# Gathering two experts' rows at once, channel-major, in a fused transformer step

## What is computed

```
def moe_ffn(h, w_rg, b_rg, w_re, b_re, w_gate, w_up, w_down):
    ...
    grp = jnp.argmax(logit_g, axis=-1)
    ...
    top_val, top_idx = lax.top_k(logit_e, TOP_K)
    weight = p_grp * jax.nn.softmax(top_val, axis=-1)
    ...
    def expert_block(args):
        tok, e, w = args
        xb = h_pad[tok]
        y = (jax.nn.silu(xb @ w_gate[e]) * (xb @ w_up[e])) @ w_down[e]
        return y * w[:, None]
```

## Time and profile before

| what | us |
|---|---|
| device time, median of 3 runs | 1075.61 |
| lowest and highest of the 3 | 1073.88, 1075.84 |
| span of the profiled execution, first to last instruction | 1073.9 |
| of it busy: TensorE matmuls | 1045.2 (97%) |
| VectorE, ScalarE, GpSimd | 285.9, 239.0, 91.3 |

### The profile page before, as it was taken

How to read it: one execution, slowest core, us unless ns; L and a number is a source line. 1 busy time by engine, 2 the same in 40 slices (tenths; PEclk the granted TensorE clock), 3 DMA queues, 4 the chain that set the end, 5 groups by cost and what they waited for, 6 DMA issues and landing times.

```text
span 1073.9 us, 14364 instructions
## 1 busy us (share of the span) xinstructions
PE 1045.2 (97%) x5798; PEld 537.2 (50%) x5798; DVE 285.9 (27%) x767; ACT 239.0 (22%) x492; POOL 91.3 (9%) x133
## 2 busy tenths in 40 slices
PE   8999999999999999999999999999999999999994
PEld 4478887555666667775543333333333333333342
DVE  1132011566333314111441111111111111122252
ACT  2011001266322243000131311111111111111153
POOL 0020040000222220000000000000000000000000
PEclk9999999999999999999999999999999999999997
DMA  9990248220545578654289999999999999999920
GB/s 330 259 300 6 79 99 177 79 80 1 168 146 160 186 272 193 248 192 161 78 329 392 379 425 426 426 428 428 427 428 427 427 428 428 426 427 424 371 73 31
DMA packets 58359, 288.93 MB, mean 269 GB/s; under 512 B 10211, under 2 KB 14540, under 8 KB 45566
## 3 DMA queue, kind: packets, MB, share of 16 engines
q1 hardware_dynamic: 48414, 259.61, 62.7%
q0 software_dynamic: 9648, 28.43, 9.1%
q10 hardware_dynamic: 240, 0.09, 0.0%
HBM read 277.87 MB, written 19.55 MB: 277 GB/s over the span
## 4 chain that ended last, share of the span: by engine, by line
PE 53%; DMA 8%; DVE 1%; issue 1%; ACT 0%; POOL 0%; SPq 0%; DVEq 0%; POOLq 0%
PE ps L1187 18%; PE ps L1215 9%; PE ps L601 9%; PE ps L1159 4%; DMA reg_o<-in_w_exp_down_dram 4%; DMA ring<-in_w_exp_up_dram 3%; PE ps L1084 3%; PE ps L672 2%; PE ps L1172 1%; PE ps L1163 1%; DMA late<-y_rows 1%; PE ps L1203 1%; PE ps L620 1%; PE ps L1055 1%; PE ps L679 1%
## 5 line engine op out<-in xcount | busy, mean ns | idle before, releaser
L1187 PE MATMUL ps<-ring,reg_xh 128*64 128x512 f32 x512 | 148.7, 595 | 2.5 <-DMA ring<-in_w_exp_up_dram 1.7
L1187 PE MATMUL ps<-late,reg_xh 128*64 128x512 f32 x336 | 148.6, 595 | 0.9 <-DMA reg_k<-in_w_exp_up_dram 0.9
L1187 PEld LDWEIGHTS ps<-ring,reg_xh 128*64 128x64 f32 x512 | 46.2, 137 | 86.9 <-issue 84.3
L2194 DVE TENSOR_TENSOR reg_xh<-reg_xh,ps 64x512 f32<-64x512 f32 x32 | 22.1, 691 | 230.4 <-ACT reg_xh L1592 230.4
L1592 ACT ACTIVATE reg_xh<-ps 64x512 f32<-64x512 f32 x32 | 34.0, 1064 | 215.0 <-PE ps L1187 215.0
L1187 PE MATMUL ps<-reg_k,reg_xh 128*64 128x512 f32 x176 | 77.8, 595 | 0.0
L2413 POOL DMA_INDIRECT y_rows<-reg_xh,slot_row x29 | 28.3, 976 | 544.4 <-ACT reg_xh L1603 503.2
L897 PE MATMUL ps<-reg_xh,ring 128*128 128x320 f32 x256 | 73.5, 436 | 0.0
L1187 PEld LDWEIGHTS ps<-late,reg_xh 128*64 128x64 f32 x336 | 44.4, 137 | 45.4 <-issue 44.9
L601 PE MATMUL ps<-reg_xh,ring 128*128 128x320 f32 x224 | 60.9, 433 | 0.0
L1159 PE MATMUL ps<-reg_xh 128*64 128x512 f32 x256 | 60.5, 592 | 0.0
(11 more groups left out here) (412 smaller groups left out, 1340.3 us busy)
## 6 DMA issues: line engine op xcount, KB each, us to landing
ring<-in_w_exp_gate_dram SPq DMA_DIRECT2D x21, 2048.0 KB, 19.4
ring<-in_w_in_dram SPq DMA_DIRECT2D x12, 2048.0 KB, 11.0
ring<-in_w_exp_down_dram SPq DMA_DIRECT2D x11, 2048.0 KB, 24.0
ring<-in_w_exp_up_dram SPq DMA_DIRECT2D x11, 2048.0 KB, 23.9
late<-in_w_exp_gate_dram SPq DMA_DIRECT2D x10, 2048.0 KB, 19.9
reg_k<-in_w_exp_up_dram SPq DMA_DIRECT2D x10, 2048.0 KB, 24.4
late<-in_w_exp_up_dram SPq DMA_DIRECT2D x10, 2048.0 KB, 23.4
reg_xh<-in_w_exp_down_dram SPq DMA_DIRECT2D x10, 2048.0 KB, 23.5
```

Source lines behind the costliest of these rows:

```text
L1187: last = pe.matmul(out[64 * part:64 * part + 64, :], xb[:, k, :], ws_[part][:, k, :], start=(k == 0), stop=(k == KT - 1))
L2194: dve.tensor_tensor(sg.rearrange("p (m q) -> p m q", m=4), sg.rearrange("p (m q) -> p m q", m=4), ps[64:128, 2 + par, :].rearrange("p (q m ...
```

## The change

The rows of two experts are gathered at once, and what was the stationary operand becomes the moving one: a block of 128 tokens x 128 channels of `xn2` is loaded, and the one-hot columns of two experts (2 x 64) stream through. The result is channel-major already, in PSUM banks 0 and 1 for both experts. `turn_rows`, the copy to `xg` and `add_rows` go. `pick` runs in every other step (par 0), before the whole of `down`, which is no longer split. VectorE builds the one-hot matrix of both experts in one instruction, into a single buffer. `times_gain` reads the two banks, one expert in each step. TensorE waits, ahead of `pick`, until both experts of the last pair have been taken out of the banks (`xe_ready`). The job `rank` moves to bank 7.

```
-    assign(proj, (1, 3, 4, 5, 2, 3))
+    assign(proj, (7, 3, 4, 5, 2, 3))
...
-            def gather(bufs, out, s_ready, count, s_done):
-
+            def pick(width, banks, s_ready, count, s_done):
 
                 pe.wait_ge(s_ready, count)
+
+                def chosen_rows(t, rows, c, m, **flags):
+
+                    c0, col = 512 * c + 128 * m, 256 * (m % 2) + 128 * c
+                    return pe.matmul(ps[:, banks[m // 2], col:col + width], xn2[rows, t, c0:c0 + 128],
+                                     sel[rows, t, :, :].rearrange("p q n -> p (q n)")[:, 0:width], **flags)
+
                 for t in range(2):
+                    for m in range(4):
+                        for c in range(2):
+                            chosen_rows(t, slice(0, 128), c, m, start=(t == 0 and m % 2 == 0 and c == 0), stop=False)
+                for m in range(2):
                     for c in range(2):
...
+                        chosen_rows(2, slice(0, 64), c, m, start=False, stop=(m == 1 and c == 1))
+                        last = chosen_rows(2, slice(64, 128), c, 2 + m, start=False, stop=(m == 1 and c == 1))
                 last.then_inc(s_done, 1)
...
-            gather(sel[0], ps[:, 0, :], sel_ready, 1, gathered)
+            pick(128, (0, 1), sel_ready, 1, picked)
             projected(1, 1)
-            pe.wait_ge(xg_added, 1)
-            turn_rows(xg_ready, 1, xg_turned)
             projected_sample()
...
-                if not last_one:
-                    gather(sel[1 - par], ps[:, 1 - par, :], sel_ready, e + 2, gathered)
+                if par == 0 and keep != 2:
+                    pe.wait_ge(xe_ready, e + 2)
+                    pick(128, (0, 1), sel_ready, i * 3 + p // 2 + 2, picked)
                 if first:
                     slot_table()
-                if not first:
-                    down(w_down, he[1 - par], ps[:, 5 - par, :], (0, 1))
-                if not last_one:
-                    pe.wait_ge(xg_added, e + 2)
-                    turn_rows(xg_ready, e + 2, xg_turned)
-                if first:
                     pe.wait_ge(sg_ready, 1)
                 else:
-                    down(w_down, he[1 - par], ps[:, 5 - par, :], (2, 3), e + 1).then_inc(down_done, 1)
+                    down(w_down, he[1 - par], ps[:, 5 - par, :], sg_count=e + 1).then_inc(down_done, 1)
                 turn_once(ps[:, 6, :]).then_inc(turned, 1)
...
-                if not last_one and keep != 2:
-                    dve.wait_ge(gathered, e + 1)
-                    select(e + 2, sel[par], 0).then_inc(sel_ready, 1)
+                if par == 0 and keep != 2:
+                    dve.wait_ge(picked, i + 1)
+                    select_pair(e + 2).then_inc(sel_ready, 1)
...
-                if not last_one:
-                    dve.wait_ge(xg_ready, e + 2)
-                    add_rows().then_inc(xg_added, 1)
-                    dve.wait_ge(xg_turned, e + 2)
-                    times_gain(xe[1 - par]).then_inc(xe_ready, 1)
+                if not last_pair:
+                    dve.wait_ge(picked, i + 2)
+                    times_gain(xe[par], par).then_inc(xe_ready, 1)
```

More of the change, by code:

```diff
@@ L252, in build @@
         ye = [reg_x[:, a:a + 512] for a in (7168, 4096)]
-        xg = reg_x[:, 3072:3584]
-        sel = [reg_x[:, 3584 + 192 * i:3776 + 192 * i].rearrange("p (t n) -> p t n", t=3) for i in range(2)]
+        sel = reg_x[:, 3584:3968].rearrange("p (t q n) -> p t q n", t=3, q=2)
         xn = reg_k[:, 0:3072].rearrange("p (t n) -> p t n", t=3)
@@ L354, in build @@
             [sem(f"ye_out{i}") for i in range(2)])
-        ov = {n: sem("more_" + n) for n in ("chunks", "sel", "gathered", "xg", "xg_turned", "xe", "up", "silu", "sg", "turned", "he",
-                                            "down", "ye", "added_rows", "stored", "out", "rows", "added")}
+        ov = {n: sem("more_" + n) for n in ("chunks", "sel", "picked", "xe", "up", "silu", "sg", "turned", "he",
+                                            "down", "ye", "stored", "out", "rows", "added")}
         rows_back = [sem(f"rows_back{i}") for i in range(3)]
@@ L1207, in rows_of, with down @@
                 return [slots[slot][:, 1024 * m:1024 * m + 1024] for m in range(4)]
-            def down(w, hb, out, rows=(0, 1, 2, 3), sg_count=None):
-                for m in rows:
+            def down(w, hb, out, sg_count=None):
+                for m in range(4):
                     for c in range(2):
@@ L1221, in _ @@
             projected(0, 1)
-            for bank in (0, 6, 7):
+            for bank in (0, 1):
                 pe.wait_ge(bank_read[bank], plan["expert loop"][bank])
@@ L1248, in expert @@
                 w_gate, w_up = EXPERT_SLOTS[p % 3][0:2]
-                first, last_one = keep == -1, keep == 3
+                first = keep == -1
                 if keep is not None and keep >= 2:
@@ L1343, in _ @@
                         n = e * EXTRA + blk + 1
-                        gather(sel[0], ps[:, 4, :], ov["sel"], n, ov["gathered"])
                         pe.wait_ge(ov["ye"], n)
-                        pe.wait_ge(ov["added_rows"], n)
-                        turn_rows(ov["xg"], n, ov["xg_turned"], 5)
+                        pick(SLOTS, (4, 5), ov["sel"], n, ov["picked"])
                         if blk == 0:
@@ L2132, in _ @@
             dve.wait_ge(gain_e_in, 16)
-            dve.wait_ge(xg_ready, 1)
-            add_rows().then_inc(xg_added, 1)
-            dve.wait_ge(xg_turned, 1)
-            times_gain(xe[0]).then_inc(xe_ready, 1)
+            dve.wait_ge(picked, 1)
+            for q in range(2):
+                times_gain(xe[q], q).then_inc(xe_ready, 1)
             for k, a_ in enumerate((a1, a2)):
```

64 lines of the change are left out of this document (21 added, 43 removed).

## The result

| what | before | after |
|---|---|---|
| device time, median of 10 runs | 1075.86 | 1078.65 |
| ratio, 95% interval | 1 | 1.0026 (1.0015 to 1.0038) |
| profiled execution: its device time | not known | 1079.56 |
| its span | 1073.9 | 1077.6 |
| TensorE matmuls busy | 1045.2 (97%) | 1028.7 (95%) |

The change makes the kernel 2.8 us slower, where +2.3 was forecast. One of the ten runs after, 1101.73 us at a lower granted clock, is left out of the ratio, and the median of the other nine is 1078.42. TensorE has 16.5 us less to do, and the time is longer.

What follows compares the result with a forecast made beforehand. The prediction took DMA to bound the expert loop, with the end following gate_up(3). A start 2.1 us later plus 0.2 for rows read back gave 1075.6 + 2.3 = 1077.9 us, range 1075.0 to 1081.0 for 8 in 10.

Steps and rivals of the forecast that it cites:

- What bounds the kernel: Expert stage: DMA bounds the loop, and its end moves one to one with the end of gate_up(3), 604.06.
- PE's time inside it is worth nothing: Expert loop: PE takes 14.04 us an expert, DMA 15.26, so PE's time there does not set the end.
- The cost of a pick: One pick on PE: 3.5 + 0.9 + 0.3 = 4.7 us, floor 4.3, ceiling 8.0.
- The sum at the start: PE's work up to gate_up(3), now with three picks: its end comes at 606.1, 2.1 us later.
- The dry stretches: DMA at 575 to 579 and 602 to 606: 266 and 138 GB/s, losing 1.5 and 2.7 us before the change.
- The small terms: Other effects besides the start: only the rows read back near the end were given a cost, +0.2 us.
- The +0.2 for the rows read back: Near the end: expert 28's scatter comes some 3 us earlier, its 1 MB competing longer with the last up matrix, +0.2 us.
- What VectorE was feared to uncover: Before gate_up(0): two times_gain of 0.69 are covered by L620 and L629, 3.8 us; without that cover, lateness adds once.
- The rival of the clock: Before the last expert: PE's longer wait lowers the clock, gate_up(31) loses 1.7 us, 0.6 hidden; +1.1, 1079.0 us. Chance 0.22.
- the forecast's own case: Whole kernel: later start 2.1 plus rows read back 0.2, +2.3 us, 1077.9 us. Chance 0.33.

Runs made afterwards that it cites:

- run 1: The kernel before, with five useless matmuls ahead of gate_up(3): 1078.20 us against 1075.39, ratio 1.0027.
- run 4: The changed kernel with one useless matmul in each of the 18 steps 6 to 23: 1078.22 us against 1075.35 for the kernel before, ratio 1.0036.
- run 2: The kernel before, with one useless matmul in each of the 18 steps 6 to 23: 1084.20 us, ratio 1.0087.
- run 3: The kernel before, with one useless matmul in each of the four steps 24 to 27: 1075.41 us against 1075.35, ratio 1.0002.
- run 8: The late pick: the changed kernel with pick and both times_gain moved into the odd step before the pair needing it; 1073.88 us against 1075.39 before, ratio 0.9997.
- run 10: As run 9, but with six useless matmuls in step 31: 1073.32 us against 1075.31 for the kernel before, ratio 0.9980.
- run 6: The changed kernel with three useless matmuls in each even step from 6 on and in steps 30 and 31: 1076.38 us, ratio 1.0013 to before.
- run 9: As run 8, with three useless matmuls in each odd step from 7 on: 1073.06 us against 1075.35 for the kernel before, ratio 0.9974.
- run 5: The changed kernel with six useless matmuls ahead of gate_up(30) and of gate_up(31): 1079.70 us against 1075.39 for the kernel before, ratio 1.0037.
- run 7: As run 6, but with six useless matmuls instead of three in steps 30 and 31: 1077.22 us against 1075.31 for the kernel before, ratio 1.0016.

## Why the prediction was right

**What bounds the kernel.** Right in its result: the load behind `gate_up(3)` moves the end one to one (run 1), and TensorE's saving in the loop is worth nothing (rows above, run 4). Two things in it were not. First, "PE's time inside it is worth nothing" holds for less work, for more work only up to 3.6 us (runs 2 and 3). The step that failed there is the rate: an expert was put at 15.26 us, worked out over the whole way to the last matrix but one, and PE's lead at 1.2 us an expert. PE's waits in the changed loop come every 30.0 us for a pair:

```profile
859.83 5.39 PE L1183 MATMUL ps<-ring,reg_xh 128*64 128x512 f32 x18 [3.36 <-DMA ring<-in_w_exp_up_dram]
889.86 1.09 PE L1183 MATMUL ps<-late,reg_xh 128*64 128x512 f32 x1 [1.96 <-DMA reg_k<-in_w_exp_up_dram]
```

so the DMA engines take 15.0 us for an expert, and PE of before was 0.95 faster, not 1.2. Over 26 experts that is 6 us, and it decides whether PE is far away from the bound or next to it. For this change it made no difference, as PE got faster. Second, the end was to hang on the down matrix of expert 30 as before, near 1004.8, which is 1003.7 for a start 1.1 earlier. It landed at 1002.41, and the chain runs over the up matrix of expert 31 instead. So the load moves the end one to one in run 1, but in the changed kernel the load is 1.6 later, the up matrix 2.4 and the down matrix 0.9.

**The cost of a pick.** Right: 4.7 forecast, 4.66 to 4.86 measured. The Trainium skill, "TensorE: Matmul & The Clock Gate", section "The mechanism" of Part 3, by whose rule a pick would have taken 8, is not borne out. If the 16 instructions on row halves cost nothing at all, 4.66 us leave 0.146 for each of the 32 full ones, where a load and its 128 columns one after the other were put at 0.22.

**The sum at the start.** +2.1 forecast for the end of `gate_up(3)`, +1.6 measured. Three terms were off by little. `down` in one piece takes 3.43 to 3.58 us, not twice 1.87: -0.5 for the two of them (the one at 577.83 took 3.43), probably since it is entered once and not twice. `slot_table` and the `turn_once` behind it took 1.86 instead of 2.18 (568.95 to the next `gate_up` at 570.81). The second and third pick took 0.16 more each, the first 0.04 less. That is -0.5 in all. The dry stretches behaved as told: loads issued at 577.87 and 604.56, where 579.1 and 606.1 were forecast with a start of the stage that came 1.1 us earlier in this execution.

**The small terms.** The +0.2 for the rows read back stays open. They were issued 8.6 us before the last up matrix landed (987.61) and before the change 6.6, as forecast in kind, and that matrix lost 0.8 us more than the load did. But the late pick issued them only 4.6 us ahead and its matrix lost 1.2, so no run here shows what the 0.8 are. From `down(30)` to the end nothing changed: 71.1 us before and 71.2 after. What VectorE was feared to uncover, it did not: `gate_up(0)` follows the side projections at 557.23 without a wait. The device time of the profiled execution is 2.0 us above its span, so the sentence ahead of the prediction that no time lies around the span is wrong. In the other kernels of this study the device time lies 1.6 to 1.7 above it where the order is the one of before (runs 1 to 3) and 2.0 where picks are used (runs 4 to 10), which may be 0.3 to 0.4 of the difference; where it comes from stays open. By the 1.7, the profiled execution of before was one of about 1075.6, near the median and not the shortest.

**The rival of the clock.** It came true in the profiled execution, together with the forecast's own case, not in its place: PE waited 4.68 us before the last up matrix (3.7 forecast) and `gate_up(31)` ran at 1.2 GHz for nearly its whole length. That costs 3.0 us, not the 1.7 that half of its length would. The forecast hid 0.6 of it behind the wait for the down matrix; but that matrix had landed at 1002.4, ahead of the 1003.45 at which a full-rate `gate_up(31)` would have ended, so nothing was hidden and its price was 3.0, not 1.1. What the Trainium skill tells in the section "HAM oscillation — how this bites in real kernels" of the same page, that a wait for the next weights lets the clock fall and the burst behind it starts at half rate, is what these rows show.

How the +2.8 adds up: the order costs some 1.9 in the profiled executions. With the clock held at 1.00 through the loop, though not always at its end, the changed kernel is at +1.0 to +1.4 (run 6), so that by this comparison some 1.5 of the 2.8 come from falls of the clock, on average over the runs; in the profiled one they were 3.0. These do not sum up exactly (1.9 is more than run 6 shows over before), and the difference of half a us is below what the runs of this study resolve. The size that was forecast is right, but in part by luck: the order cost some 0.4 less than 2.3, and the clock, which the forecast had left out of its sum with a chance of 0.22, made up for it.

## What to carry to other kernels

Before taking work off an engine, ask what its last wait was for and how far behind its feeder it runs; an engine at 97% may be neither the bound nor have any room. Where loads are released by the consumer, its work before the first releases is what counts: order it so that nothing stands there which is only needed later (here that alone, run 8, took the changed kernel back to the time before). And TensorE made faster than its feeder waits longer, and can then run the burst that matters at half rate; work that is useless but short, kept in the waits, came out 0.8 to 2.5 us ahead (runs 6 and 9 against the same kernels without it), at the edge of what the runs resolve.

## What the runs showed of the hardware

The length of a wait does not settle whether the clock falls. In the changed kernel the granted clock fell to 0.50 behind waits of 3.31, 3.36, 1.96 and 4.68 us, and stayed at 1.00 behind waits of 2.45 and 3.24; in run 8 it fell behind waits of 1.94, 2.41 and 3.38 and stayed behind 1.95 and 3.33. Two waits of the same length, first the changed kernel's at 949.84, then one of run 5, each with the stretch behind it:

```profile
949.84 7.09 PE L1183 MATMUL ps<-ring,reg_xh 128*64 128x512 f32 x32 [3.24 <-DMA ring<-in_w_exp_up_dram]
```

```profile
951.00:957.00 6.00, 6.00 (x29) 2.21 (x26) 0.00 (x0) 0.04 (x1) 0.00 (x0) 1.00 1.01 429
```

```profile
919.74 0.61 PE L1183 MATMUL ps<-ring,reg_xh 128*64 128x512 f32 x1 [3.24 <-DMA late<-in_w_exp_up_dram]
```

```profile
919.00:925.00 6.00, 5.26 (x18) 2.04 (x20) 0.00 (x0) 0.00 (x0) 0.00 (x0) 0.72 1.01 425
```

These are two programs. That one program also differs from one execution to the next is what run 5's two groups and their clocks show.

The router just ahead of the experts has such a place too. It ends in small matmuls with short waits, and the eight instructions of the side projection behind them took 5.21 us before (542.51 to 547.72), at a granted clock of 0.57, and 3.5 in run 6, at 1.00. The program up to there is the same in all of them; of the twelve profiles three have the short form (runs 2, 6 and 7). The stretch of 542 to 546 in the two, before first:

```profile
542.00:546.00 4.00, 4.00 (x10) 1.93 (x10) 2.32 (x16) 1.01 (x2) 0.00 (x0) 0.57 1.02 430
```

```profile
542.00:546.00 4.00, 4.00 (x13) 1.97 (x12) 2.05 (x11) 1.19 (x2) 0.00 (x0) 1.00 0.98 418
```

The first pick then starts at 546.5 in runs 6 and 7, and at 548.3 to 550.8 in the other profiles of the changed kernels. So 1.7 us can come or go ahead of the experts, close to the size of the effect under study, and it is one reason why executions are compared above from the first pick on.
